# Causal masks, gain column sums and six groups of query products moved ahead in the two sparse-attention layers

## The chip, the core and the metric

One core of a Trainium2 chip runs the whole network in one launch. The metric is the device time of that core in microseconds (us). TensorE is called PE in the profile (PEld is its weight load), VectorE is DVE, ScalarE is ACT, GpSimd is POOL, and SP issues the DMAs.

## What is computed

The network has one layer of a first kind (local attention, pooling, gated feed-forward) and then two layers of a second kind. The change touches only the second kind. For 256 tokens of width 1024, cut to what matters:

```
proj = h @ w_in                      # qa, kva, kr, dq, dk, dv, iq, ik, iw
# multi-head latent attention, 8 heads of 64 + 32
q = rms_norm(qa) @ w_q_up            # rotary on the last 32
k_nope, v = rms_norm(kva) @ w_uk, rms_norm(kva) @ w_uv
out_a = softmax(mask(q k^T * 96**-0.5)) v
# sparse attention, 8 heads of 64, keys chosen by an indexer
score = sum over 8 index heads of iw * relu(iq ik^T * 32**-0.5)
score = where(key <= query, score, -inf);  sel = top_k(score, 64)
out_b = softmax(dq dk[sel]^T * 64**-0.5 - slope * distance) dv[sel]
x = layer_norm(ALPHA * x + [out_a, out_b] @ w_o)
# 16 experts, 2 of them for each token, chosen by sigmoid(x @ router_w)
x = layer_norm(ALPHA * x + experts(x))
```

`dq` is `h @ w_in[:, dq columns]`: these are the query products of the change. The router needs, for each expert, the sum over the features of gain times router weight and of shift times router weight: the column sums.

## The kernel before

Each engine has its own program, written out by hand, and semaphores order them. `w.next(name)` waits for one more count of a semaphore, `wait_ge` for a fixed count. Tokens stand in two halves of 128 rows. Weights come as float32 slabs, which ACT splits into a high part (`hi`) and DVE or POOL into a low part (`lo`); each product of two float32 numbers is then three fp32r matmuls (`products`, lines 2083 to 2087).

In each of the two layers PE does the following.

- It multiplies the input by `w_in` (`token_major`, slabs L_IN and L_IN_B), ACT and DVE save the result to `proj`, and PE turns the normalised latents (`feature_major`, line 2024: four chunks of 128 columns ahead, the fifth when the products reach it; a turn is a transposition with the identity, line 2010).
- It multiplies the latents by `w_q_up` (slabs L_QUP), `w_uk` and `w_uv`. Beside these run the turns of the indexer's inputs (`turn_b`) and the 16 score products of the indexer (`idx_score`, line 2379). ACT takes the relu of each (`idx_relu`, line 1028), and DVE adds it up into `score`, whose tile is `bias_h` (`idx_add`, line 1786).
- It turns `q_up` (tile `wide_a`) and `k_up` (tile `wide_b`) in four rounds of four plus four turns. ACT copies the queries to `q_t` (line 1058), DVE the keys to `k_t` (line 1815). A round's query turn waits for the query copy two rounds back, and its key turn for the key copy two rounds back.
- It computes the column sums, 8 matmuls of 128 x 32 in float32 (line 2413; in the trace x16, two passes each). DVE adds the causal masks to both halves of `score` (line 1820).
- It runs the first attention in 19 steps: step i issues the scores of unit i (line 2164), the flip of unit i-2, which is a turn of its probabilities, the weighing of unit i-3 (line 2180) and then what is put beside. A unit is a head and a half; units 0 to 7 have 128 keys, units 8 to 15 have 256. From step 4 on the query products for the second, sparse attention stand beside (`sparse_queries`): 32 groups of three matmuls with 256 columns, 2 or 3 groups in each step, written to banks 6 and 7.
- Each unit also costs DVE a round: `largest` (MAX8, line 1831), `logits` (line 1311) and `take` (line 1836). Eight rounds of largest and take choose the 64 keys of a half.
- Then come the sparse attention, the output projection, the router and the experts.

Who waits for whom at the change: `logits(i)` needs the score on PE; the exponential (line 849) needs the logits; flip i needs the exponential; weighing i needs ACT's copy of the turned probabilities (line 858), and ACT does that copy of unit i only after the exponential of unit i+2. POOL makes `router_gb` (router weight times gain and shift, line 719), which the column sums read.

Of the kernel before, what the change touches and what calls it, by code (L numbers as in the profile page):

```python
# [30 lines left out]
ALU = mybir.AluOpType  # L31
AX = mybir.AxisListType

P = 128
SEQ, D = 256, 1024
# [213 lines left out]
def build(nc, A, out):  # L249

    ctx = ExitStack()
    with ctx:
# [228 lines left out]
        N_IDX = HALVES * IDX_HEADS  # L481

# [155 lines left out]
        def _(pool):  # L638
# [42 lines left out]
            for layer in range(LAYERS):  # L681
                if layer == 0:
                    pool.wait_ge(S["x_updated"], 8)
                else:
                    pool.wait_ge(S["ln_done"], HALVES * layer)
                nc.gpsimd.memset(q_up[:, :, :, MLA_D:P], 0.0).then_inc(S["pads_zero"], 1)
# [29 lines left out]
                pool.wait_ge(S["columns_in"], 16)  # L716
                pool.wait_ge(S["router_in"], 16 * N_ROUTER)
                for g in range(2):
                    nc.gpsimd.tensor_tensor(router_gb[:, g], router_w[:],
                                            columns[:, layer, 0, g, :].unsqueeze(2).broadcast_to([P, DC, EXPERTS]), ALU.mult)  # L720
# [24 lines left out]
        def _(act):  # L745
# [253 lines left out]
            for layer in range(LAYERS):  # L999
# [31 lines left out]
                def save_qup(i):  # L1031
# [5 lines left out]
                              low=True, to=low_x)  # L1037
                splits_to(b + L_UK)
# [22 lines left out]
                w.next("gain_sums")  # L1061
                nc.scalar.copy(route[:, 4, :], bank[6][:, sums_at])
# [165 lines left out]
        def _(dve):  # L1228
# [520 lines left out]
            for layer in range(LAYERS):  # L1749
# [53 lines left out]
                w.next("idx_masked")  # L1803
                for i in range(N_IDX):
                    idx_add(i)
                    if i + 1 == IDX_AFTER_QUP:
                        save_qup(1)
# [197 lines left out]
        def _(pe):  # L2005
# [320 lines left out]
            for layer in range(LAYERS):  # L2326
# [20 lines left out]
                def turn_b(at):  # L2347

                    w.upto(("copied_even", "copied_odd")[at % 2], (4, 2)[at % 2] * layer + at // 2)
# [8 lines left out]
                def qup_first():  # L2358

                    groups[0] += 1  # L2360
                    if groups[0] == HALVES * QC // 2:
                        w.next("in_saved0", 3)
                        w.next("in_saved1", 3)
# [4 lines left out]
                def idx_score():  # L2368
# [3 lines left out]
                    if i == 0:  # L2372
                        w.next("copied_even", 2)
# [7 lines left out]

# [369 lines left out]
```

## Time and profile before

| what | value |
|---|---|
| median of 3 runs | 1110.01 us (1109.86 to 1110.74) |
| profiled execution | 1114.11 us |
| its span | 1112.2 us |
| PE busy | 1061.4 us, 95% of the span |
| DVE, ACT, POOL busy | 558.0, 437.5, 116.8 us |
| chain that ended last | PE 83%, DVE 6%, DMA 6%, ACT 3%, issue 2% |
| mean granted clock of PE | 0.976 |

The span is the time from the first instruction to the last of one execution; the device time of that execution is a little longer. All times of stretches and instructions below count from the span's start. A granted clock of 1.0 stands for 2.4 GHz, 0.5 for 1.2 GHz.

### The profile page before, as it was taken

The numbers are of one execution on the slowest core, as the hardware profiler recorded it, in microseconds if no ns is written. First come the engines' busy times: TensorE is split into PE (matmuls) and PEld (weight loads), VectorE is DVE, ScalarE is ACT, GpSimd is POOL, SyncE is SP. The second block draws the span as 40 slices with busy tenths as digits, with TensorE's granted clock in tenths as the row PEclk, the third lists the DMA queues.
The fourth block names the chain that finished last, engine by engine and source line by source line (L and its number), as shares of the span: only waits on it lengthen the run. The fifth ranks groups of instructions, "written<-read, shape, count | busy, mean of one in ns | idle before, by whom it ended". The sixth has DMA issues, their size and how long they took to land.

```text
span 1112.2 us, 16375 instructions
## 1 busy us (share of the span) xinstructions
PE 1061.4 (95%) x6290; PEld 741.5 (67%) x6290; DVE 558.0 (50%) x1071; ACT 437.5 (39%) x811; POOL 116.8 (11%) x129
## 2 busy tenths in 40 slices
PE   8999998999999998999999999989999999999995
PEld 5898987999999797886344443349797734444332
DVE  5764376676666667657322223265765642222224
ACT  5345454554554356644211121145555522112111
POOL 1200000000000025340000000022534000000000
PEclk9999998999999998999999999989899999999998
DMA  8843245555555354358999999935444989999993
GB/s 300 272 141 127 77 152 189 169 172 189 190 187 187 111 172 185 119 181 354 423 420 421 420 422 420 420 130 184 138 167 126 403 363 420 422 420 420 422 420 139
DMA packets 84877, 294.60 MB, mean 265 GB/s; under 512 B 6376, under 2 KB 45638, under 8 KB 60106
## 3 DMA queue, kind: packets, MB, share of 16 engines
q1 hardware_dynamic: 81936, 289.33, 68.1%
q10 hardware_dynamic: 2874, 4.36, 1.1%
q8 instruction: 44, 0.72, 0.3%
q14 instruction: 23, 0.19, 0.0%
HBM read 292.62 MB, written 1.05 MB: 264 GB/s over the span
## 4 chain that ended last, share of the span: by engine, by line
PE 83%; DVE 6%; DMA 6%; ACT 3%; issue 2%; SPq 0%; DVEq 0%; POOL 0%; ACTq 0%
PE bank L2569 17%; PE bank L2578 9%; PE bank L2085 8%; PE bank L2086 7%; PE bank L2087 7%; PE bank L2146 4%; PE bank L2148 4%; PE bank L2147 4%; PE bank L2010 4%; DMA raw<-in_w_in 3%; PE bank L2556 3%; DMA early_w<-in_w_up 3%; PE bank L2180 2%; PE bank L2601 2%; PE bank L2164 2%
## 5 line engine op out<-in xcount | busy, mean ns | idle before, releaser
L1236 DVE TENSOR_TENSOR lo<-raw,hi 128x2048 fp32r<-128x2048 f32 (+4 forms) x73 | 155.5, 2138 | 47.0 <-ACT hi L753 46.7
L753 ACT CAST hi<-raw 128x2048 fp32r<-128x2048 f32 (+5 forms) x74 | 132.1, 1791 | 45.2 <-PE bank L2087 41.4
L1488 DVE TENSOR_TENSOR proj<-bank,proj 64x512 f32<-64x512 f32 x32 | 34.6, 1082 | 210.4 <-PE bank L2591 210.4
L2146 PE MATMUL bank<-xs,hi 128*128 128x256 f32 x448 | 129.0, 288 | 3.6 <-DVE xs L1270 1.5
L2148 PE MATMUL bank<-xs,lo 128*128 128x256 f32 x448 | 127.9, 286 | 0.0
L2147 PE MATMUL bank<-xs,hi 128*128 128x256 f32 x448 | 127.9, 286 | 0.0
L2085 PE MATMUL bank<-hi,xs 128*128 128x512 f32 (+2 forms) x240 | 90.3, 376 | 4.7 <-DVE xs L1274 1.6
L1165 ACT ACTIVATE proj<-bank 64x512 f32<-64x512 f32 x32 | 18.8, 589 | 191.4 <-PE bank L2570 191.4
L2146 PEld LDWEIGHTS bank<-xs,hi 128*128 128x128 f32 x448 | 87.3, 195 | 5.0 <-issue 3.4
L2087 PE MATMUL bank<-lo,xs 128*128 128x512 f32 (+2 forms) x240 | 87.9, 366 | 0.0
L2086 PE MATMUL bank<-hi,xs 128*128 128x512 f32 (+2 forms) x240 | 87.8, 366 | 0.0
L2147 PEld LDWEIGHTS bank<-xs,hi 128*128 128x128 f32 x448 | 87.3, 195 | 0.4
L2148 PEld LDWEIGHTS bank<-xs,lo 128*128 128x128 f32 x448 | 87.2, 195 | 0.0
L658 POOL TENSOR_TENSOR lo<-raw,hi 128x512 fp32r<-128x512 f32 (+1 forms) x44 | 57.1, 1328 | 279.4 <-ACT hi L753 217.3
L2570 PE MATMUL bank<-moe_w,xg 128*64 128x512 f32 x160 | 70.3, 592 | 0.0
L1506 DVE SCALAR_TENSOR_TENSOR expert_out<-bank,slot_gate,expert_out 128x512 fp32r<-128x512 f32 x32 | 24.0, 750 | 88.7 <-ACT expert_out L1178 88.7
L649 POOL TENSOR_TENSOR stat<-stat,power 128x1 f32<-128x1 f32 (+2 forms) x15 | 16.5, 1098 | 476.7 <-DVE stat L1967 227.0
L1178 ACT ACTIVATE expert_out<-bank,slot_gate 128x512 fp32r<-128x512 f32 x32 | 22.0, 687 | 109.9 <-PE bank L2578 109.9
L1723 DVE SCALAR_TENSOR_TENSOR proj<-bank,conv,proj 128x255 f32<-128x255 f32 (+1 forms) x88 | 38.5, 478 | 49.3 <-ACT proj L977 46.4
L2578 PE MATMUL bank<-moe_w,act_t 128*64 128x512 f32 x256 | 59.8, 601 | 0.9 <-ACT act_t L1169 0.9
L849 ACT ACTIVATE prob<-logit,row_min 128x128 f32<-128x128 f32 (+1 forms) x80 | 36.5, 456 | 46.7 <-DVE row_min L1311 45.0
L2085 PEld LDWEIGHTS bank<-hi,xs 128*128 128x128 f32 x240 | 45.2, 188 | 10.8 <-issue 2.8
(306 smaller groups left out, 2398.0 us busy)
## 6 DMA issues: line engine op xcount, KB each, us to landing
raw<-in_w_up SPq DMA_DIRECT2D x34, 1024.0 KB, 5.1
moe_w<-in_w_down SPq DMA_DIRECT2D x32, 1024.0 KB, 19.5
raw<-in_w_in SPq DMA_DIRECT2D x20, 1024.0 KB, 5.6
moe_w<-in_w_up SPq DMA_DIRECT2D x20, 1024.0 KB, 20.9
raw<-in_w_down SPq DMA_DIRECT2D x19, 1024.0 KB, 5.1
early_w<-in_w_gate SPq DMA_DIRECT2D x12, 1024.0 KB, 18.7
early_w<-in_w_up SPq DMA_DIRECT2D x12, 1024.0 KB, 20.8
raw<-in_w_gate SPq DMA_DIRECT2D x10, 1024.0 KB, 16.2
```

What stands on the lines that cost most here:

```text
L658: ins = nc.gpsimd.tensor_tensor(low(n)[:, part], raw[:, n % RING, part], high(n)[:, part].bitcast(F32), ALU.subtract)
L753: nc.scalar.copy(high(n)[:, 0:size], raw[:, n % RING, 0:size]).then_inc(S["hi_done"], 1)
L1236: tt(low(n)[:, 0:size], raw[:, n % RING, 0:size], high(n)[:, 0:size].bitcast(F32), ALU.subtract).then_inc(S["lo_done"], 1)
L2085: mm(out_, lhs_hi, rhs_hi, start=first, stop=False)
L2086: mm(out_, lhs_lo, rhs_hi, start=False, stop=False)
L2087: return mm(out_, lhs_hi, rhs_lo, start=False, stop=last)
L2146: mm(dst, wh[:, k, col], x_hi, start=k == 0, stop=False)
L2147: mm(dst, wh[:, k, col], x_lo, start=False, stop=False)
L2148: ins = mm(dst, wl[:, k, col], x_hi, start=False, stop=k == k_chunks - 1)
L2569: mm(to[0:SLOTS, :], rows_[:, kk, :], gate[:, k, :], start=kk == 0, stop=kk == DC - 1)
L2570: ins = mm(to[SLOTS:P, :], rows_[:, kk, :], up[:, k, :], start=kk == 0, stop=kk == DC - 1)
L2578: ins = mm(to[SLOTS * c:SLOTS * (c + 1), :], act[:, kk, :], down[:, k, 512 * c:512 * (c + 1)], start=kk == 0, stop=kk == 3)
```

## The change

Four things move, in each of the two layers.

1. **Column sums.** PE issues them between the fourth and the fifth chunk of the latents' turns, ahead of the products with `w_q_up`; ACT copies them to `route` after the latents' copies and not after the query copies. POOL makes `router_gb` at the start of the layer, ahead of its memsets. The waits for `in_saved0`, `in_saved1` and `pads_zero` move with them.
2. **Causal masks.** DVE adds the first half's mask inside the indexer's additions, after the one with i = 8, and the second half's after round 1 of the first attention.
3. **Six groups of query products** stand among the turns: three after round 2 and three after round 3.
4. **The other 26 groups** stand beside steps 1 to 17 of the first attention, one or two in each, and none in step 18. The wait for the last relu, which stood ahead of the column sums, now stands ahead of the first turn.

```
+        GROUPS_BY_TURN = (0, 0, 3, 6)
POOL, start of a layer:
+                pool.wait_ge(S["columns_in"], 16)
+                pool.wait_ge(S["router_in"], 16 * N_ROUTER)
+                for g in range(2):
+                    nc.gpsimd.tensor_tensor(router_gb[:, g], router_w[:],
+                                            columns[:, layer, 0, g, :].unsqueeze(2).broadcast_to([P, DC, EXPERTS]), ALU.mult)
                 nc.gpsimd.memset(q_up[:, :, :, MLA_D:P], 0.0).then_inc(S["pads_zero"], 1)
...
ACT, after feature_major(QC + KVC, ...):
+                w.next("gain_sums")
+                nc.scalar.copy(route[:, 4, :], bank[6][:, sums_at]).then_inc(S["copied_even"], 1)
                 splits_to(b + L_UK)
...
DVE:
+                def causal(half):
+                    dst = score[:, half, 0:P * (half + 1)]
+                    tt(dst, dst, mask[:, half, 0:P * (half + 1)], ALU.add).then_inc(S["idx_masked"], 1)
                 for i in range(N_IDX):
                     idx_add(i)
+                    if i == IDX_HEADS:
+                        causal(0)
...
-                for half in range(HALVES):
-                    keys = P * (half + 1)
-                    dst = score[:, half, 0:keys]
-                    tt(dst, dst, mask[:, half, 0:keys], ALU.add).then_inc(S["idx_masked"], 1)
-                w.next("idx_masked", HALVES)
                 def largest(i):
+                    if i % HEADS == 0:
+                        w.next("idx_masked")
                 def take(i):
+                    if i == 1:
+                        causal(1)
...
PE:
+                w.next("in_saved0", 3)
+                w.next("in_saved1", 3)
+                w.next("pads_zero", 2)
+                for k in range(DC):
+                    ins = mm(bank[6][:, sums_at]..., router_gb[:, :, k, :], start=k == 0, stop=k == DC - 1)
+                ins.then_inc(S["gain_sums"], 1)
                 token_major(b + L_QUP, 1, QC, [4 * MLA_D], qup[0], lhs=low_x, ready=fm_chunk, between=qup_first)
...
                 w.next("idx_relu", N_IDX)
                 for i in range(4):
                     for src, to, copied in ((q_up, q_turned(i), "copied_q"), (k_up, k_turned(i), "copied_k")):
...
+                    sparse_queries(GROUPS_BY_TURN[i])
...
                 attention(...,
-                          beside=lambda i: sparse_queries(i) if i > 3 else None)
+                          beside=lambda i: sparse_queries(6 + 26 * i // 17 if i < 17 else 2 * 2 * DC))
```

The number given to `sparse_queries` is now how many groups have been issued in all; before, it was `2 * 2 * DC * (i - 3) // 15`, thus 2 groups at a step and 3 at steps 11 and 18.

On PE, before: the last two rounds of turns (`wide_a` queries, `wide_b` keys), the column sums and the first scores (`k_t,q_t`).

```order
L2010 MATMUL bank<-const,wide_b 128x128 [waits copied_k]
L2010 MATMUL bank<-const,wide_b 128x128 x3
L2010 MATMUL bank<-const,wide_a 128x128 [waits copied_q]
L2010 MATMUL bank<-const,wide_a 128x128 x3
L2010 MATMUL bank<-const,wide_b 128x128 [waits copied_k]
L2010 MATMUL bank<-const,wide_b 128x128 x3
L2413 MATMUL bank<-router_gb,const 128x32 [waits idx_relu,kv_saved1,kv_saved0]
L2413 MATMUL bank<-router_gb,const 128x32 x7
L2164 MATMUL bank<-k_t,q_t 128x128 [waits copied_k,copied_q]
L2164 MATMUL bank<-k_t,q_t 128x128
L2164 MATMUL bank<-k_t,q_t 128x128 [waits logits]
```

On PE, now: round 3's key turn is followed by three groups of query products (`xs,hi` and `xs,lo`), and then by the first score.

```order
L2015 MATMUL bank<-const,wide_b 128x128 [waits copied_k]
L2015 MATMUL bank<-const,wide_b 128x128 x3
L2090 MATMUL bank<-xs,hi 128x256
L2091 MATMUL bank<-xs,lo 128x256
L2092 MATMUL bank<-xs,hi 128x256
L2090 MATMUL bank<-xs,hi 128x256
L2091 MATMUL bank<-xs,lo 128x256
L2092 MATMUL bank<-xs,hi 128x256
L2090 MATMUL bank<-xs,hi 128x256
L2091 MATMUL bank<-xs,lo 128x256
L2092 MATMUL bank<-xs,hi 128x256
L2169 MATMUL bank<-k_t,q_t 128x128 [waits copied_q,copied_k,kv_saved1,kv_saved0]
```

Three more groups stand ahead of round 3 in the same way, and the column sums are gone from here. On PE, before, at the latents' turns (`const,xn`) ahead of the products with `w_q_up` (`hi,low_x`):

```order
L2010 MATMUL bank<-const,xn 128x128 [waits fm_lo]
L2010 MATMUL bank<-const,xn 128x128 x3
L2010 MATMUL bank<-const,xn 128x128 [waits fm_lo,lo_done]
L2010 MATMUL bank<-const,xn 128x128
L2085 MATMUL bank<-hi,low_x 128x384 [waits fm_lo]
```

and now:

```order
L2015 MATMUL bank<-const,xn 128x128 [waits fm_lo]
L2015 MATMUL bank<-const,xn 128x128 x3
L2389 MATMUL bank<-router_gb,const 128x32 [waits pads_zero,in_saved1,in_saved0]
L2389 MATMUL bank<-router_gb,const 128x32 x7
L2015 MATMUL bank<-const,xn 128x128 [waits fm_lo,lo_done]
L2015 MATMUL bank<-const,xn 128x128
L2090 MATMUL bank<-hi,low_x 128x384 [waits fm_lo]
```

The column sums (`router_gb,const`) stand between the fourth and the fifth chunk. On DVE, before, from the key copies to the first logits (`bias_h<-bias_h,const` are the masks, ISA is the logits' instruction):

```order
L1815 COPY k_t<-bank 128x512 [waits turned_a,idx_added]
L1815 COPY k_t<-bank 128x512 [waits turned_a] x3
L1820 TENSOR_TENSOR bias_h<-bias_h,const 128x128
L1820 TENSOR_TENSOR bias_h<-bias_h,const 128x256
L1831 MAX power<-bias_h 128x8 [waits idx_masked]
L1311 ISA logit,row_min<-bank,const 128x128 [waits probs,scores]
```

and now:

```order
L1824 COPY k_t<-bank 128x512 [waits turned_a,idx_added]
L1824 COPY k_t<-bank 128x512 [waits turned_a] x3
L1834 MAX power<-bias_h 128x8 [waits idx_masked]
L1312 ISA logit,row_min<-bank,const 128x128 [waits probs,scores]
```

No mask addition is left between the last key copy and the first largest.

## Rows read from the trace of the kernel before

**Rows 1.** The page, part 2: granted clock of TensorE in 40 slices, tenths.
```profile
PEclk9999998999999998999999999989899999999998
```

**Rows 2.** Busy time in stretches: both turn-and-attention stages, their slow parts, experts.
```profile
core 0: us, PE busy (x) PEld busy (x) DVE busy (x) ACT busy (x) POOL busy (x), PEclk, DMA share, GB/s
424.80:462.56 37.76, 34.25 (x250) 32.02 (x248) 26.82 (x97) 22.40 (x68) 16.16 (x14) 0.91 0.51 196
791.47:830.93 39.46, 37.17 (x250) 34.87 (x248) 26.32 (x97) 22.29 (x68) 16.10 (x14) 0.83 0.50 187
434.40:441.30 6.90, 6.40 (x29) 5.80 (x29) 4.27 (x26) 4.12 (x18) 0.00 (x0) 0.52 0.97 383
796.40:810.00 13.60, 13.15 (x60) 12.20 (x58) 8.03 (x36) 6.55 (x21) 3.49 (x3) 0.50 0.83 311
520.00:526.00 6.00, 6.00 (x29) 2.03 (x30) 5.68 (x17) 1.44 (x2) 0.00 (x0) 1.00 0.42 122
526.00:730.00 204.00, 201.14 (x1054) 80.91 (x1050) 53.77 (x102) 39.02 (x73) 0.15 (x1) 1.00 1.01 419
```

**Rows 3.** Timeline of PE, layer 0: start, duration, instructions, [idle before <-releaser].
```profile
402.50 1.25 PE L2010 MATMUL bank<-const,xn 128*128 128x128 f32 x10
404.94 0.44 PE L2085 MATMUL bank<-hi,low_x 128*128 128x384 f32 x1 [1.18 <-DVE low_x L1274]
...
429.19 0.66 PE L2010 MATMUL bank<-const,wide_b 128*128 128x128 f32 x4 [1.21 <-DVE k_t L1815]
429.69 0.60 PE L2010 MATMUL bank<-const,wide_a 128*128 128x128 f32 x4
...
430.56 1.87 PE L2413 MATMUL bank<-router_gb,const 128*128 128x32 f32 x16
432.27 0.69 PE L2164 MATMUL bank<-k_t,q_t 128*128 128x128 f32 x4
434.13 0.49 PE L2164 MATMUL bank<-k_t,q_t 128*128 128x128 f32 x2 [1.18 <-DVE row_min L1311]
```

**Rows 4.** Timeline of PE, layer 0, inside the first attention.
```profile
439.33 0.63 PE L2164 MATMUL bank<-k_t,q_t 128*128 128x128 f32 x2
...
441.60 0.38 PE L2164 MATMUL bank<-k_t,q_t 128*128 128x128 f32 x2
...
442.07 0.37 PE L2085 MATMUL bank<-xs,hi 128*128 128x256 f32 x1
...
442.87 0.39 PE L2164 MATMUL bank<-k_t,q_t 128*128 128x128 f32 x2
...
449.70 0.36 PE L2085 MATMUL bank<-xs,hi 128*128 128x256 f32 x1
...
450.85 0.60 PE L2164 MATMUL bank<-k_t,q_t 128*128 128x256 f32 x2
```

**Rows 5.** Timeline of PE, layer 1: the fourth turn of the queries.
```profile
796.37 0.95 PE L2010 MATMUL bank<-const,wide_a 128*128 128x128 f32 x4
```

**Rows 6.** Timeline of DVE, layer 0: indexer, key copies, masks, first rounds.
```profile
419.80 0.92 DVE L1786 SCALAR_TENSOR_TENSOR bias_h<-logit,idx_w,bias_h 128x256 f32<-128x256 f32 x1 [0.77 <-ACT logit L1028]
...
428.45 1.29 DVE L1815 COPY k_t<-bank 128x512 f32<-128x512 f32 x2
...
431.37 2.19 DVE L1820 TENSOR_TENSOR bias_h<-bias_h,const 128x128 f32<-128x128 f32 x2
433.59 0.29 DVE L1831 MAX8 power<-bias_h 128x8 f32<-128x128 f32 x1
...
434.38 0.29 DVE L1831 MAX8 power<-bias_h 128x8 f32<-128x128 f32 x1
```

**Rows 7.** All instructions of line 1820 (mask additions): ns minimum/median/maximum.
```profile
L1820 DVE TENSOR_TENSOR bias_h<-bias_h,const x4: 411/1003/1483, 431.4 to 800.0; 128x128 f32<-128x128 f32 x2, 128x256 f32<-128x256 f32 x2
```

**Rows 8.** Timeline of ACT, layer 0: the last relu of the indexer.
```profile
425.87 0.41 ACT L1028 ACTIVATE logit<-bank 128x256 f32<-128x256 f32 x1
```

**Rows 9.** Timeline of POOL, layer 0: after its three memsets.
```profile
396.55 1.01 POOL L649 TENSOR_TENSOR stat<-stat,power 128x4 f32<-128x4 f32 x1 [18.45 <-DVE stat L1257]
```

More of the change, by code:

```diff
@@ L715, in _ @@
                     .then_inc(S["kr_spread"], 1)
[L716 to L720, printed above, removed]
                 w.next("qup_saved0", 2)
@@ L1060, in _ @@
                     w.skip("turned_a")
-                w.next("gain_sums")
-                nc.scalar.copy(route[:, 4, :], bank[6][:, sums_at])
                 def sparse_queries(i):
@@ L2347, in turn_b @@
                 def turn_b(at):
-                    w.upto(("copied_even", "copied_odd")[at % 2], (4, 2)[at % 2] * layer + at // 2)
+                    w.upto(("copied_even", "copied_odd")[at % 2], (5 * layer + 1, 2 * layer)[at % 2] + at // 2)
                     for c in range(2):
@@ L2361, in qup_first @@
                     if groups[0] == HALVES * QC // 2:
-                        w.next("in_saved0", 3)
-                        w.next("in_saved1", 3)
                         w.next("staged", 6)
@@ L2372, in idx_score @@
                     if i == 0:
-                        w.next("copied_even", 2)
+                        w.next("copied_even", 3)
                         w.next("copied_odd", 2)
@@ L2398, in _, with sparse_queries @@
                 w.next("kr_spread")
-                w.next("pads_zero", 2)
-                for i in range(4):
-                    for src, to, copied in ((q_up, q_turned(i), "copied_q"), (k_up, k_turned(i), "copied_k")):
-                        w.upto(copied, 4 * layer + i - 1 if i else 0)
-                        for c in range(2):
-                            for half in range(HALVES):
-                                at = c * SEQ + half * P
-                                ins = turn(to[:, at:at + P], src[:, half, 2 * i + c, :])
-                        ins.then_inc(S["turned_a"], 1)
-                w.next("kv_saved0")
-                w.next("kv_saved1")
-                w.next("idx_relu", N_IDX)
-                for k in range(DC):
-                    ins = mm(bank[6][:, sums_at].rearrange("p (g e) -> p g e", g=2), const[:, C_ONE:C_ONE + 1].broadcast_to([P, P]),
-                             router_gb[:, :, k, :], start=k == 0, stop=k == DC - 1)
-                ins.then_inc(S["gain_sums"], 1)
-                w.next("copied_q", 4)
-                w.next("copied_k", 4)
+                w.next("idx_relu", N_IDX)
                 asked = [0]
-                def sparse_queries(i):
-                    groups_by = 2 * 2 * DC * (i - 3) // 15
+                def sparse_queries(groups_by):
                     while asked[0] < groups_by:
@@ L2435, in sparse_queries @@
                             ins.then_inc(S["slab_used"], 1)
+                for i in range(4):
+                    for src, to, copied in ((q_up, q_turned(i), "copied_q"), (k_up, k_turned(i), "copied_k")):
+                        w.upto(copied, 4 * layer + i - 1 if i else 0)
+                        for c in range(2):
+                            for half in range(HALVES):
+                                at = c * SEQ + half * P
+                                ins = turn(to[:, at:at + P], src[:, half, 2 * i + c, :])
+                        ins.then_inc(S["turned_a"], 1)
+                    sparse_queries(GROUPS_BY_TURN[i])
+                w.next("kv_saved0")
+                w.next("kv_saved1")
+                w.next("copied_q", 4)
+                w.next("copied_k", 4)
                 attention(lambda h, half: q_t[:, h, half * P:(half + 1) * P],
```

2 lines of the change are left out of this document (added).

## The prediction

> **What bounds the kernel now.** I read the page first, then the stretches, then the timelines of the engines around the change. On the page the reader is to see TensorE's granted clock dip in a few slices of an otherwise full row [rows 1]. The stretches tell where: in each layer from the first turn of `q_up` to the first score of the sparse attention, 37.76 us in layer 0 and 39.46 us in layer 1 [rows 2]. Inside them the clock is 0.52 for 6.90 us in layer 0 and 0.50 for 13.60 us in layer 1, that is 1.2 in place of 2.4 GHz. PE counts as busy for 34.25 and 37.17 us there, DVE for 26.8 and 26.3, ACT for 22.4 and 22.3. So PE's own stream sets the length, plus its waits, plus what the low clock costs.
>
> The waits lie early [rows 3]. The third round's key turn waits 1.21 us for DVE's key copy; the third score, at 434.13, waits 1.18 us for the logits, since DVE does both masks (2.19 us) before the first largest [rows 6]; and no product group is there to fill until step 4. With the narrow column sums (430.56 to 432.27) this makes ten microseconds in which the array does little.
>
> After these stages come the experts, fed by weights at 419 GB/s with the DMA engines at 1.01 [rows 2]. That looks like a cover under which a gain could vanish. It is not: from 520 to 526 us the DMAs run at 0.42, 122 GB/s, because all slots are full and wait for PE. The stream starts again when PE starts the experts, so what PE gains before carries through.
>
> **The change part by part, on PE, for one layer.** I build up the length of the stretch anew.
>
> (a) First turn to end of round 2: 4.9 us, as before. Before it is 424.80 to 429.69 and 791.47 to 796.37 [rows 2, 3, 5]. The wait for the last relu now stands ahead of the first turn, and that relu ends at 426.28 [rows 8], 1.5 us after the first turn of now. It costs nothing, for the round-2 key turn waits anyway for DVE's first key copy, started at 428.45 after the last addition [rows 6]; a set of four turns takes 0.44 (two sets from 429.69 to 430.56), so the five sets ahead of that key turn, begun at 426.3, end at 428.5, still before the copy does. Without that cover it would cost up to 1.5.
>
> (b) Three groups, round 3, three groups. Three groups take 1.15 us (449.70 to 450.85), two take 0.80 (442.07 to 442.87) [rows 4], thus 0.355 a group and 0.09 a burst. Round 3 takes 0.87 [rows 3]. Sum 3.17. The last key copy of DVE (0.69, half of the 1.29 for two) is hidden by the second three.
>
> (c) Steps 0 to 4. A step of 128 keys without its groups is 441.60 to 442.07, 0.47: score 0.22, flip 0.11, weighing 0.14. Five scores, three flips and two weighings are 1.7 us, the six groups in four bursts 2.5. Then there is a wait: weighing 0 needs ACT's copy, which stands behind the exponential of unit 2. From the first score, DVE needs about 0.43 to the first logits, two rounds of 0.79 (433.59 to 434.38) and the second half's mask, 0.41 at its shortest [rows 6, 7], with the next largest and logits 0.5; ACT adds some 0.9. That is 3.8 us, against 2.5 of work that PE has until there. I take 1.4 of waiting; the bounds are 0.5 (DVE's parts overlap PE's) and 2.5. Sum 5.6.
>
> (d) Steps 5 to 18. Steps 6 to 18 took 441.60 to 462.56, 20.96 us at full clock with 28 groups in 13 bursts. Now they hold 19 in 12: less 9 x 0.355 and 0.09, 17.7. Step 5 with one group is 0.9. Sum 18.6.
>
> (e) Waits of the leaner steps. A step with one group of 128 keys is 0.91, hardly longer than DVE's 0.79, and DVE also saves the first half's heads in between. DVE's 26.8 us of work must now fit in some 33. I take 1.0, from bounds 0 (it all fits) and 2.0.
>
> The stretch becomes 4.9 + 3.2 + 5.6 + 18.6 + 1.0 = 33.3 us.
>
> (f) Column sums, new place. The latents' turns end at 403.75 and the product waits 1.18 us for `low_x` [rows 3]. The sums take 1.71 us (430.56 to 432.27), start when eight of the ten turns are out, and push the last two and the product to about 405.3 from 404.94: 0.4 us, from bounds 0 and 1.7. Behind PE here stand ACT's and DVE's copies of the fifth chunk, then the splits of `w_uk`: 0.8 us later in the worst case, while their slab is first needed some ten microseconds on. ACT's small copy of the sums (0.2) is in the same gap.
>
> (g) First mask inside the additions: DVE stands idle 0.77 us before the next addition [rows 6], and and that addition takes 0.92 while POOL rotates. I take 0, from bounds 0 and 1.1 (half of the 2.19 for two).
>
> (h) POOL's two products ahead of its memsets: after the memsets POOL is idle for 18.45 us [rows 9]; nothing. In layer 0 they wait for a small load (128 x 64 numbers) that SP issues right after the first kind of layer ends; the same idle time covers it. SP's later loads wait for low parts and turns that move with PE.
>
> So layer 0 goes from 37.76 to 33.7, a gain of 4.1, and layer 1 from 39.46 to 33.7, a gain of 5.7: together 9.8 us. The sum is made against the profiled execution (1114.11 us, span 1112.2), which is 4.1 us above the median of the runs; taken from the median, 1110.0 - 9.8 = **1100.2 us**. Roughly half of it is waiting that is filled; the rest is that 20 us at half clock disappear. That last part is a choice. Before each fall of the clock PE had issued turns with waits between, and in layer 0 then the column sums and the first scores; the clock rose again after the products came back, at 441.3 and 810.0. Now two bursts of three groups stand there.
>
> A rule speaks against counting on this. The row first: in layer 1 the clock had fallen by 796.4, and ahead of it stood turns with no wait longer than 1.2 us. The Trainium skill, "TensorE: Matmul & The Clock Gate", table "Why this matters for your kernels", asks only that long idle gaps between bursts be avoided; by it the clock would never have fallen here, and the trace disagrees. The same page, "Part 4: PE-mode transpose", says that a transposition does not count as PE work for the clock in the way a matmul does. By that rule the trace agrees, and it is the second rival below: the turns of (a) are all still there.
>
> **The rivals.**
>
> *B. The clock still falls among the turns.* For: (a) keeps its turns and its waits, and in layer 1 the fall came before any of the new groups. Against: in layer 0 it came only at 434.4, long after such turns, so some products nearby are enough to hold it. Price: a step with two groups took 439.33 to 441.60, 2.27, at the low clock, 1.27 at the full one [rows 4]; a slow stretch of 6.90 us full of products so costs 3.0. In one layer 1103.2, in both 1106.2 us.
>
> *C. The chain of the softmax, not PE, is the length.* If units pass at DVE's and ACT's pace, 26 groups beside run no faster than 32 did, and the six ahead only push the first score: 3.2 us after round 2 in place of 2.6 (429.69 to 432.27), plus the 0.4 of (f), thus 1.0 later in each layer. Result 1112.1, slower. It decides if steps 5 to 18 shrink by less than 1 us. Against: from step 6 on PE is never idle before.
>
> *D. The gain is given back.* The weight stream ends when it did, since the slots' loads take their time from something that did not move. Result 1110.0. Against: the 0.42 from 520 to 526. That the change does not do what it says is no case: the order on PE shows the groups and sums moved.
>
> **How the numbers follow.** Forecast 0.58; B 0.28 (mostly in one layer); C 0.04; D 0.06; the rest, 0.04, is a gain above the bounds. Within the forecast, (c), (e) and (f) at their good ends give 2.3 us a layer more, at their bad ends 2.8 less; they will not all fall on one side, so I take some 3 us down and 4 up, and B reaches to 1106.2: range 1097.0 to 1106.5. A measurement of this kernel can tell 0.2%, 2.2 us, from no change. Faster by more: 0.90. Within: 0.06. Slower: 0.04.
>
> **What would show it.** In the profile after: the two stretches at about 33.7 us each; a granted clock of 1.0 through both; column sums right behind eight latents' turns, with the product after them 0.4 us late; no wait for `k_t` after round 3; one wait of about 1.4 us at the first weighing; the sparse attention's first score right behind the last weighing; experts of the same length as before. It is wrong if a stretch shows 0.5 for several microseconds (B), if steps 5 to 18 show waits for `row_min` or `prob_t` of more than 2 us in sum (C), or if the experts start early and end as late as before (D).

## The result and the profile after

The change makes the kernel faster: a median of 1104.19 us over six runs (1101.22 to 1105.70), beside 1110.6 us for the kernel before (six runs, 1109.86 to 1116.77). The ratio is 0.9921, with a 95% interval of 0.9903 to 0.9940. The forecast was 1100.2 with a range of 1097.0 to 1106.5. The profiled execution of the changed kernel took 1101.22 us, its span is 1099.4.

On the page of the changed kernel PE is busy for 1050.7 us, 96% of the span (before 1061.4), DVE for 556.7, ACT for 437.7, POOL for 117.3. Its row of the clock answers to [rows 1]: no slice but the last is below nine tenths.

```profile
PEclk9999999999999999999999999999999999999998
```

From here on I measure each layer from a mark that lies ahead of the turns and of all that changed its order behind them: from the start of the indexer's last six scores to the first score of the sparse attention. Only the column sums and the first mask now stand ahead of that mark. The first turn stands 1.61 us behind that mark before. These are the two stretches before, and below them the section between them (columns as in [rows 2]):

```profile
423.19:462.56 39.37, 35.82 (x256) 33.03 (x254) 28.28 (x98) 23.77 (x71) 17.77 (x15) 0.91 0.49 188
789.87:830.93 41.06, 38.73 (x256) 35.88 (x254) 27.43 (x98) 23.65 (x71) 17.70 (x15) 0.83 0.48 180
462.56:789.87 327.31, 317.61 (x1704) 173.40 (x1703) 133.78 (x296) 102.05 (x215) 36.55 (x47) 0.98 0.82 329
```

The same of the changed kernel, and with them the end of the routing and the experts of layer 0:

```profile
424.05:458.47 34.42, 31.62 (x239) 28.45 (x238) 26.32 (x97) 23.86 (x71) 16.61 (x14) 1.00 0.57 215
784.16:818.49 34.33, 31.60 (x239) 28.43 (x238) 25.99 (x97) 23.88 (x71) 16.62 (x14) 1.00 0.59 215
458.47:784.16 325.69, 316.25 (x1718) 174.30 (x1719) 134.25 (x297) 102.07 (x216) 37.84 (x48) 0.99 0.83 331
516.00:522.00 6.00, 6.00 (x30) 2.00 (x30) 5.76 (x17) 1.31 (x2) 0.00 (x0) 1.00 0.44 126
522.00:726.00 204.00, 201.12 (x1054) 80.89 (x1050) 53.70 (x102) 38.84 (x73) 0.00 (x0) 1.00 1.01 418
```

The reader is to see three things. The granted clock is 1.00 in both stretches, where it was 0.91 and 0.83. The stretches are 4.95 and 6.73 us shorter, 11.7 together; the column sums, which left them, cost 0.41 a layer at their new place, so the two layers bring 10.9 us. The spans of this pair differ by 12.8 us. The rest, 1.9 us, is less than what executions of one kernel differ by outside these stretches: the section between them took 327.31 us before and 325.69 now, and in a second execution of each kernel (both in the experiments) 324.93 before and 328.01 now. Last, the experts [rows 2] took 204 us then and now, and the DMAs ran at 0.44 and 126 GB/s just ahead of them: the gain of layer 0 went through.

In the timeline of PE after, layer 0, around the turns and the first units, compare [rows 3]:

```profile
405.64 0.42 PE L2015 MATMUL bank<-const,xn 128*128 128x128 f32 x2
...
424.05 1.77 PE L2382 MATMUL bank<-gates 128*128 128x256 f32 x6
427.27 0.63 PE L2015 MATMUL bank<-const,wide_a 128*128 128x128 f32 x4 [1.46 <-ACT logit L1029]
...
430.03 0.66 PE L2015 MATMUL bank<-const,wide_b 128*128 128x128 f32 x4 [0.38 <-DVE k_t L1824]
430.44 0.36 PE L2090 MATMUL bank<-xs,hi 128*128 128x256 f32 x1
...
433.54 0.65 PE L2169 MATMUL bank<-k_t,q_t 128*128 128x128 f32 x4
...
436.83 0.43 PE L2185 MATMUL bank<-value,prob_t 128*128 128x64 f32 x2 [0.57 <-ACT prob_t L859]
...
438.78 0.39 PE L2169 MATMUL bank<-k_t,q_t 128*128 128x128 f32 x2
```

PE now waits 1.46 us for the last relu ahead of the first turn. The wait for a key copy is down to 0.38 us, from 1.21. The third score follows the first two with one group between them and no wait, where it waited 1.18. At the first weighing PE waits 0.57.

### The profile page after: what moved, and what is told of

It reads as the page before. It is cut to its first block, busy times and chain, and to the rows that moved or that the text cites. A ratio compares the mean times of both kernels' runs of the same rounds, so it can differ in the third digit from the quotient of the medians.

```text
span 1099.4 us, 16372 instructions
## 1 busy us (share of the span) xinstructions
PE 1050.7 (96%) x6286; PEld 731.1 (66%) x6290; DVE 556.7 (51%) x1071; ACT 437.7 (40%) x811; POOL 117.3 (11%) x129
## 4 chain that ended last, share of the span: by engine, by line
PE 71%; DMA 5%; DVE 5%; issue 1%; ACT 1%; SPq 0%; DVEq 0%; ACTq 0%
PE bank L2574 17%; PE bank L2583 9%; PE bank L2090 6%; PE bank L2091 6%; PE bank L2092 6%; PE bank L2151 4%; PE bank L2153 4%; PE bank L2152 4%; PE bank L2015 3%; PE bank L2561 3%; DMA raw<-in_w_in 3%; DMA early_w<-in_w_up 3%; PE bank L2606 2%; PE bank L2185 2%; PE bank L2169 2%
```

## The experiments

A stretch below is the one just defined, a pair of numbers is layer 0 and layer 1, and the clock is the one granted in it. All kernels compute the whole result. What is called masks, sums and groups are the three parts of the change: the causal masks moved into the additions and rounds; the column sums moved ahead of the product with `w_q_up`; six groups placed among the turns and 26 beside the units from the first on.

| kernel | median us | ratio to before, 95% | stretches us | clock |
|---|---|---|---|---|
| before (profiled first) | 1110.01 | | 39.37 / 41.06 | 0.91 / 0.83 |
| before, once more | 1110.18, one execution | | 38.98 / 39.49 | 0.91 / 0.91 |
| the change | 1104.19 | 0.9921 [0.9903, 0.9940] | 34.42 / 34.33 | 1.00 / 1.00 |
| the change, once more | 1103.30 | 0.9904 [0.9882, 0.9926] | 34.42 / 34.36 | 1.00 / 1.00 |
| masks only | 1115.24 | 0.9999 [0.9977, 1.0021] | 38.71 / 41.15 | 0.91 / 0.83 |
| sums only | 1113.17 | 0.9983 [0.9967, 0.9999] | 40.22 / 39.10 | 0.83 / 0.91 |
| masks and sums | 1108.89 | 0.9938 [0.9920, 0.9956] | 35.79 / 37.20 | 1.00 / 0.95 |
| groups only | 1105.49 | 0.9912 [0.9885, 0.9938] | 36.49 / 36.41 | 1.00 / 1.00 |
| masks and groups | 1107.67 | 0.9936 [0.9910, 0.9962] | 36.51 / 36.40 | 1.00 / 1.00 |
| sums and groups | 1103.10 | 0.9899 [0.9870, 0.9929] | 35.04 / 34.95 | 1.00 / 1.00 |
| before with idle matmuls | 1108.40 | 0.9952 [0.9933, 0.9971] | 37.39 / 37.30 | 1.00 / 1.00 |
| no groups among the turns | 1103.10 | 0.9906 [0.9879, 0.9934] | 34.34 / 34.24 | 1.00 / 1.00 |
| first groups in the key wait | 1101.45 | 0.9886 [0.9859, 0.9913] | 33.55 / 33.44 | 1.00 / 1.00 |
| and groups by step | 1100.56 | 0.9875 [0.9844, 0.9905] | 33.03 / 32.95 | 1.00 / 1.00 |

Each ratio is taken against executions of the kernel before that ran beside that kernel, and these were not alike: their median is 1114.14 us for masks, sums, both and groups alone, 1113.02 for the idle matmuls, the two versions with groups at other places ("no groups among the turns", "first groups in the key wait") and the change once more, and 1113.68 for the rest. That is why 1115.24 goes with 0.9999. The medians alone don't order the kernels: executions of the changed kernel scatter by 4.5 us, of the kernel before by 7, of "masks only" by 10. A stretch at full clock repeats within 0.03 us (34.42 and 34.42, 34.33 and 34.36), so differences below a microsecond are read from the stretches.

**Masks only.** Of the change, only this part, in the kernel before:

```
 for i in range(N_IDX):
     idx_add(i)
+    if i == IDX_HEADS:
+        causal(0)
...
-for half in range(HALVES):
-    ... tt(dst, dst, mask[:, half, 0:keys], ALU.add)
-w.next("idx_masked", HALVES)
...
 def take(i):
     ...
+    if i == 1:
+        causal(1)
```

> The kernel before with only the causal masks moved. Theory A (three things stand ahead of the attention and end within a microsecond of each other: PE's column sums, DVE's masks, ACT's table load, which follows the copy of the sums): the masks alone give at most 0.3 us a layer, since the first exponential still waits for the table load until 433.9; time within 1 us of before, and the clock falls as before. Theory B (the masks were what the first scores waited for, 1.2 us): 1.2 us less in each layer, about 2.4 us faster.

Measured: ratio 0.9999, stretches within 0.7 us of before's, the clock as before. DVE was free earlier, but its work found the next engine busy. ACT in layer 0 of this kernel (start, duration, instruction):

```profile
434.23 0.18 ACT L1062 COPY route<-bank 128x32 f32<-128x32 f32 x1 [1.56 <-PE bank L2420]
434.42 1.28 ACT L849 ACT_TABLE_LOAD   x1
435.71 0.40 ACT L849 ACTIVATE prob<-logit,row_min 128x128 f32<-128x128 f32 x1
```

ACT can't load the exponential's table before it has copied the column sums, and those come last on PE. The load takes 1.28 us, and PE's first flip waits 0.88 for the exponential behind it. A wait for DVE has become one for ACT.

**Sums only.** The column sums and their copy at the new place, masks, turns and groups as before (the relu wait back behind the turns, groups from step 4 on):

```
-    sparse_queries(GROUPS_BY_TURN[i])
...
-beside=lambda i: sparse_queries(6 + 26 * i // 17 if i < 17 else 2 * 2 * DC)
+beside=lambda i: sparse_queries(2 * 2 * DC * (i - 3) // 15) if i > 3 else None
...
+causal(0)
+causal(1)
+w.next("idx_masked", HALVES)
```

> The kernel before with only the column sums moved ahead of the query-latent products. Theory A: PE is ready for the first score earlier but DVE is not (masks end at 433.6); the stretch gains nothing and 0.4 us is added ahead of it: 0 to 1 us slower than before in all. Theory B (PE's stream is the length, so 1.71 us of sums leaves it and 0.4 comes back): 1.3 us less in each layer, about 2.6 us faster.

Measured: ratio 0.9983, at most 0.3% of gain, where a little loss was expected. Now the masks hold: between the last key copy and the first logits on DVE the two take 1.30 us in layer 0 and 2.18 in layer 1, and there PE waits 1.85 us for the logits. At the full clock of its layer 1 the part ahead of the attention is 8.42 us, 0.66 shorter than the 9.08 in layer 0 of before. The product with `w_q_up` starts 2.85 us behind the latents' first turn, 2.44 before: the new place costs 0.41.

**Masks and sums,** that is the change without its groups (the second diff without its last three lines).

> Masks and column sums moved, the query products as before (from step 4). Theory A: together they free the start of the attention, first score to fifth score 0.8 to 1.7 us earlier in each layer; the clock still falls in at least one layer, since nothing wide stands there: 1.5 to 3.5 us faster than before, and the groups are worth the other 4 to 6 us of the change. Theory C (the groups are worth little): as fast as the changed kernel within 1 us.

Measured: ratio 0.9938, some 7 us, twice the upper end of what was expected. Neither part did much alone; together they bring a stretch of 35.79 at full clock:

```profile
425.89:461.68 35.79, 31.97 (x240) 28.67 (x238) 26.45 (x97) 23.58 (x70) 17.73 (x15) 1.00 0.56 207
789.15:826.35 37.20, 33.38 (x239) 30.16 (x238) 26.10 (x97) 23.58 (x70) 17.72 (x15) 0.95 0.53 199
```

And with no group of products before step 4 the clock held in layer 0; in layer 1 it fell only 12 us behind the mark, for some 3.5 us.

**Groups only.** Turns and groups as in the change, masks as before. The sums stay behind the turns, but in bank 7 on PE and ACT, since bank 6 now holds products of a group:

```
-    nc.scalar.copy(route[:, 4, :], bank[6][:, sums_at])
+    nc.scalar.copy(route[:, 4, :], bank[7][:, sums_at])
...
+w.next("idx_relu", N_IDX)
...
         ins.then_inc(S["turned_a"], 1)
+    sparse_queries((0, 0, 3, 6)[i])
```

> The query products moved as in the change, column sums (in bank 7) and masks at their old places. Theory A: the clock holds through both stretches and the products fill; the masks' 2.2 us on DVE and the sums' 1.7 us on PE stay ahead of the first scores, so each stretch is 1.5 to 2.5 us longer than in the changed kernel: 4 to 6 us faster than before. Theory C: within 2 us of before.

Measured: ratio 0.9912, stretches 36.49 and 36.41 at full clock. The stretches are longer than the change's by what was expected; the gain over before, 9 to 10 us, is larger than the 4 to 6 expected. This part alone carries most of what a median shows. The two parts that did next to nothing in the kernel before are worth another 2.1 us of the stretch with it, 1.7 net of the sums' 0.41.

**Before with idle matmuls.** The order of the work is untouched, but for the relu wait, which now stands ahead of the key turn of round 2; bf16 matmuls on zeros into bank 7, whose result nobody reads, fill PE's waits:

```
+    if i == 2 and src is k_up:
+        w.next("idx_relu", N_IDX)
+        busy(5, bank[7])
     w.upto(copied, 4 * layer + i - 1 if i else 0)
...
+busy(2, bank[7])
 w.next("kv_saved0")
 w.next("kv_saved1")
-w.next("idx_relu", N_IDX)
...
-beside=lambda i: sparse_queries(i) if i > 3 else None)
+beside=lambda i: sparse_queries(i) if i > 3 else busy((0, 4, 2, 2)[i], bank[7]))
```

> The kernel before with nothing moved, but idle matmuls of 512 bf16 columns on zeros in PE's waits: 5 ahead of the round-2 key turn, 2 after the turns, and 4, 2 and 2 beside steps 1 to 3 of the first attention (bank 7, not read). Theory A (half of the change's gain is the clock, held by wide matmuls in this place): granted clock 1.0 in both stretches, layer 1's stretch 3 to 5 us shorter, layer 0's 1 to 2.5, in all 3 to 6 us faster than before. Theory B (the clock is not governed by what stands here): the clock falls as before, 0 to 2 us slower.

Measured: ratio 0.9952. The stretches of this kernel, then the first burst of layer 0 (the trace has four of its five matmuls) and the key turn behind it, which no longer waits:

```profile
425.10:462.49 37.39, 35.81 (x268) 31.78 (x269) 28.28 (x98) 23.76 (x71) 17.76 (x15) 1.00 0.53 198
788.58:825.88 37.30, 35.73 (x269) 31.79 (x270) 27.93 (x98) 23.77 (x71) 17.77 (x15) 1.00 0.53 198
```
```profile
429.94 1.03 PE L2201 MATMUL bank<-zeros 128*128 128x512 bf16 x4
431.10 0.66 PE L2010 MATMUL bank<-const,wide_b 128*128 128x128 f32 x4
```

Work that computes nothing takes 1.98 and 3.76 us off the stretches. So whether the clock falls in them hangs on what PE does in its early waits. This run doesn't tell whether it is the waiting that costs the clock or the lack of such matmuls: both changed at once. Some 0.4 us of the idle work lands on the path (the first score comes 9.50 us behind the mark, 9.08 before), so the order of before at full clock is 37.0 to 37.4 us. With it the two shares of this pair of profiles separate: of 10.9 us, the clock gave some 2.0 to 2.4 in layer 0 and 3.8 to 4.1 in layer 1; the order of the work gave 2.2 to 2.6 in each.

**No groups among the turns.** The change with all 32 groups beside the steps:

```
-GROUPS_BY_TURN = (0, 0, 3, 6)
+GROUPS_BY_TURN = (0, 0, 0, 0)
...
-beside=lambda i: sparse_queries(6 + 26 * i // 17 if i < 17 else 2 * 2 * DC)
+beside=lambda i: sparse_queries(2 * 2 * DC * (i + 1) // 18 if i < 17 else 2 * 2 * DC)
```

> The changed kernel without the six groups among the turns: all 32 groups beside steps 0 to 17, one or two in each. Theory A (the groups' gain is that they begin before step 4 at all, and the clock): steps 0 to 3 now take them and the turns lose 2.3 us, so the stretch is the same within 0.5 us if the clock holds; if it falls in layer 1, as it did behind the turns before, 2 to 3.5 us are lost there. Theory D (the place among the turns matters by itself): 1 to 2 us longer in each layer at full clock.

Measured: ratio 0.9906, and the stretches are those of the change, 0.1 us shorter:

```profile
422.27:456.61 34.34, 31.32 (x240) 28.33 (x238) 26.35 (x97) 23.88 (x71) 16.62 (x14) 1.00 0.59 216
782.84:817.08 34.24, 31.21 (x240) 28.32 (x238) 25.99 (x97) 23.89 (x71) 16.61 (x14) 1.00 0.58 216
```

The two bursts of three groups among the turns, which the diff shows most prominently, are neither needed for the clock nor do they save anything. The first score comes 1.1 us earlier without them, and the attention takes 1.0 longer.

**First groups in the key wait.** The last relu and the first three groups stand between the query and the key turn of round 2, so that the relu wait no longer holds the first turn and the groups fill the wait for the key copy:

```
-w.next("idx_relu", N_IDX)
...
+            if i == 2 and src is k_up:
+                w.next("idx_relu", N_IDX)
+                sparse_queries(GROUPS_BY_TURN[2])
...
-    sparse_queries(GROUPS_BY_TURN[i])
+    if i == 3:
+        sparse_queries(GROUPS_BY_TURN[3])
```

> The changed kernel with the relu wait moved behind the first five turn sets and the first three groups put between the query and the key turns of round 2, where PE waited for the key copy. Theory A (PE's stream plus its waits is the length; POOL's low part of the slab is there in time): 0.8 to 1.2 us shorter in each layer, 1.6 to 2.4 us faster than the changed kernel. Rival: the low part or the relu holds the groups and with them the key turn, so DVE's last copies come later and nothing is gained, or 0.5 us is lost.

Measured: ratio 0.9886, the stretches 0.87 and 0.89 us shorter than the change's, all of it ahead of the first score (8.59 us behind the mark, not 9.49).

**The change once more,** for the scatter.

> The changed kernel once more, to see where its runs differ (1101.2 to 1105.7). Theory A: the turn-and-attention stretches are the same within 0.3 us at full clock; what differs is the granted clock, in one of these stretches or at the transitions (before the first layer's end, before the experts, between the layers), 1 to 4 us. Rival: the difference is in the weight stream of the experts at full clock.

Measured: 1103.30 us, ratio 0.9904, the stretches within 0.03 us. The section between the two stretches and the window from 720 to 740 us in it, here and then in the first profile:

```profile
457.48:785.49 328.01, 317.32 (x1718) 174.90 (x1719) 135.00 (x297) 102.14 (x216) 37.88 (x48) 0.98 0.82 328
720.00:740.00 20.00, 16.74 (x67) 7.43 (x64) 11.17 (x25) 8.05 (x10) 7.89 (x11) 0.74 0.37 131
```
```profile
720.00:740.00 20.00, 15.82 (x75) 7.62 (x77) 12.93 (x30) 9.75 (x13) 8.37 (x11) 0.91 0.43 155
```

The section is 2.3 us longer than in the first profile, and the clock in the window is 0.74, not 0.91: executions of one kernel differ by where the clock falls outside these stretches.

**Masks and groups; sums and groups.** The first is "groups only" with the first diff; the second is the change with `causal(0)` and `causal(1)` behind the key copies.

> Masks and groups moved, column sums at their old place (bank 7). Theory A (the sums' 1.71 us lie on PE's stream, and the table load behind their copy holds the first exponential; the masks matter only once the sums are gone): the stretch from the indexer's last six scores to the sparse attention is as long as with the groups alone, 36.4 us, within 0.3. Rival (the masks are worth their 1.2 us of waiting by themselves): 35.2 to 35.6.

> Column sums and groups moved, masks at their old place behind the last key copy. Theory A: the two mask additions (0.8 to 2.2 us on DVE, by how much POOL still runs) now hold the first logits, while one group fills only 0.4: the stretch is 34.9 to 36.0 where the changed kernel has 34.4. Rival (the groups hide the masks): 34.4 within 0.2.

Measured, layer 0 of each, masks and groups first:

```profile
425.87:462.38 36.51, 33.40 (x256) 30.22 (x254) 26.46 (x97) 23.99 (x72) 16.64 (x14) 1.00 0.54 203
```
```profile
422.85:457.89 35.04, 31.80 (x240) 28.45 (x238) 27.31 (x98) 23.89 (x71) 16.62 (x14) 1.00 0.57 211
```

At full clock throughout, the parts can be priced. With the sums at their old place, moving the masks is worth 0.0 (36.49 and 36.51); with them moved, 0.6 (35.04 to 34.42). Moving the sums is worth 2.1 of the stretch if the masks are moved (36.51 to 34.42) and 1.45 if not (36.49 to 35.04), less the 0.41 in each. Of the 2.1, 1.72 is PE time ahead of the first score (11.21 to 9.49 us) and the rest is the table load: in "groups only", too, it stands behind the copy of the sums and the first exponential starts 1.7 us after the first score (436.10 and 434.41), where it takes 0.8 in the change (434.34 and 433.54).

**Groups by step.** The kernel of "first groups in the key wait", with the other 26 groups spread by hand, more of them where PE waited:

```
+BY_STEP = (0, 1, 4, 0, 1, 1, 2, 1, 2, 1, 2, 1, 2, 1, 2, 2, 2, 1, 0)
...
-beside=lambda i: sparse_queries(6 + 26 * i // 17 if i < 17 else 2 * 2 * DC))
+beside=lambda i: sparse_queries(6 + sum(BY_STEP[:i + 1])))
```

> As the version with groups in the round-2 wait, and the other 26 groups by a table: four at step 2 and none at step 3, two at step 15 and one at step 17, to fill the waits of 0.57 us at the first weighing and 0.27 at the fourteenth. Theory A: 33.0 to 33.3 us a stretch in place of 33.5; time 0.4 to 1 us less, which runs whose clock differs elsewhere may hide. Rival: four groups at step 2 hold score 3 and with it DVE, 33.5 or more.

Measured: median 1100.56 us, ratio 0.9875 [0.9844, 0.9905], stretches 33.03 and 32.95. These are all of PE's waits from the first turn to step 5 of layer 0:

```profile
430.10 0.66 PE L2016 MATMUL bank<-const,wide_a 128*128 128x128 f32 x4 [0.62 <-ACT q_t L1062]
...
431.05 0.36 PE L2091 MATMUL bank<-xs,hi 128*128 128x256 f32 x1 [0.29 <-POOL lo L660]
...
438.97 0.44 PE L2186 MATMUL bank<-value,prob_t 128*128 128x64 f32 x2 [0.29 <-ACT prob_t L860]
```

Of 33.03 us PE is busy for 31.70; little is left to fill here. By its stretches it beats the change by 1.4 us in each layer; the intervals of the two ratios overlap, so the medians alone don't show it.

**Before once more,** one execution.

> The kernel before once more. Theory A (its two stretches differ from run to run only by where the clock falls, with everything else repeating): a stretch without a fall of the clock would be 37.2 to 37.5 us; with 6.8 us at half clock 39 to 40, with 13.6 us about 41; its time lies 6 to 12 us over the changed kernel's. Rival: the stretches differ at the same clock.

Measured: 1110.18 us; the stretches and the section between them:

```profile
423.64:462.62 38.98, 35.48 (x256) 32.85 (x255) 28.30 (x98) 23.77 (x71) 17.78 (x15) 0.91 0.51 190
787.55:827.04 39.49, 35.91 (x256) 33.08 (x255) 27.96 (x98) 23.76 (x71) 17.80 (x15) 0.91 0.50 187
462.62:787.55 324.93, 314.50 (x1701) 172.37 (x1702) 132.79 (x296) 102.04 (x215) 36.54 (x47) 0.99 0.83 331
```

The low clock comes back in both layers, but in layer 1 it lasts much less long than in the execution on which the prediction was built (0.91, not 0.83), and the stretch is 1.57 us shorter.

## Why the prediction was right, and where it was not

The forecast case came true: faster by more than 0.2%, the clock at 1.00 in both stretches, experts of the same length. Its terms, against the trace of the changed kernel, layer 0. The first turn would have come at 425.66, had it not waited for the relu (the mark, 424.05, plus the 1.61 of before).

| term | predicted | measured |
|---|---|---|
| (a) first turn to end of round 2 | 4.9 | 425.66 to 430.44, 4.78 |
| (b) two bursts and round 3 | 3.17 | 430.44 to 433.54, 3.10 |
| (c) steps 0 to 4 | 5.6 | 433.54 to 438.78, 5.24 |
| (d), (e) steps 5 to 18 and their waits | 19.6 | 438.78 to 458.47, 19.69 |
| sum | 33.3 | 32.81 |
| (f) column sums at the new place | 0.4 | 0.41 |

**(a)** The relu wait did stand on PE for 1.46 us, and it did cost nothing: the key turn of round 2, which waited 1.21 us before [rows 3], now waits 0.38. DVE's key copies set that point. "First groups in the key wait" shows what was left on the table: with the groups in that wait the same part is 0.9 shorter.

**(c)** The wait at the first weighing is 0.57 us, not the 1.4 taken, near the low bound of 0.5. The terms of the chain that were too large can be read on DVE and ACT:

```profile
433.27 0.28 DVE L1834 MAX8 power<-bias_h 128x8 f32<-128x128 f32 x1
434.00 0.29 DVE L1312 CUSTOM_DVE_ANT_0 logit<-bank,const 128x128 f32<-128x128 f32 x1 [0.44 <-PE bank L2169]
...
435.28 0.42 DVE L1809 TENSOR_TENSOR bias_h<-bias_h,const 128x256 f32<-128x256 f32 x1
```
```profile
432.83 1.28 ACT L850 ACT_TABLE_LOAD   x1
434.34 0.40 ACT L850 ACTIVATE prob<-logit,row_min 128x128 f32<-128x128 f32 x1 [0.22 <-DVE row_min L1312]
...
436.53 0.24 ACT L859 COPY prob_t<-bank 128x128 f32<-128x128 f32 x1
```

The first logits start 0.46 us after the first score (433.54), as taken. The third start at 435.81, after two rounds and the mask: 1.81, where the sum had 1.99. From there to the weighing at 436.83 it is 1.02, where "the next largest and logits 0.5; ACT adds some 0.9" made 1.4, since ACT's parts overlap DVE's. That is 3.29 us in place of 3.8, and PE's work in it is 2.72 in place of 2.5. The table load isn't on this chain: it stands at 432.83 now, behind the last query copy, and is over when the logits come. The prediction priced the move of the sums on PE alone and never named this load. It is why the move of the sums is worth more than PE's 1.7 us, and why the masks are worth nothing without it; the sum came out right since (c) was built up anew, from scratch, for the order in which all parts are there.

**(d) and (e)** The one named wait of PE behind step 5 is 0.27 us; what the leaner steps cost beyond that can't be told from PE's work in the trace. Together they are 0.1 off.

**(g)** The first mask takes 0.71 us in layer 1, and the next addition starts as it ends:

```profile
779.64 0.35 DVE L1784 TENSOR_SCALAR bias_h<-logit,idx_w 128x256 f32<-128x256 f32 x1 [0.42 <-ACT logit L1029]
780.03 0.71 DVE L1809 TENSOR_TENSOR bias_h<-bias_h,const 128x128 f32<-128x128 f32 x1
780.69 0.99 DVE L1787 SCALAR_TENSOR_TENSOR bias_h<-logit,idx_w,bias_h 128x256 f32<-128x256 f32 x1
```

It fits the 0.77 us gap [rows 6]: 0, as taken. **(h)** POOL's two products and memsets run from 377.94 us on, and no wait for `pads_zero` shows: 0, as taken.

**The gain, taken from the median.** Here the prediction went wrong, by a step of its own: "taken from the median, 1110.0 - 9.8". The 9.8 was worked out against an execution of 1114.11 us, and from there it would have given 1104.3, beside the 1104.19 measured. The 1110.0 was the median of three executions, and they were short ones: of the 40 executions of the kernel before that ran beside the experiments, on three chips, 39 took longer (1109.84 to 1116.97 us); whether the chip or chance made the first three short stays open. Against its share of the 40, the change once more brought 0.9904, some 10.7 us. A part of the 9.8, of the 5.7 in layer 1 above all, was the time at low clock of the profiled execution. "Before once more" ran in 1110.18 with a layer 1 that had 1.57 us less to lose and a layer 0 with 0.39 less; its stretches against the change's, less 0.41 each, give 8.9 us, not 10.9. So the size of the gain was right within what the clock of the kernel before varies by, and the number was 4 us low because it started too low. That 1104.19 still lies in the range is luck: no term of the range stands for the starting point, and its room upward was taken for bad ends of the terms and for rival B, none of which came. The bad ends of (c), (e) and (f) also add up to 3.4 us a layer (1.1, 1.0 and 1.3), not to 2.8; nothing came near them.

**Why the clock holds.** That the clock would hold came true, but not for the reason given, that "two bursts of three groups stand there". Those bursts aren't needed: without them, with the groups beginning beside step 0, the clock is 1.00 as well ("no groups among the turns"). What the runs show is a count. In the nine profiles with query products before step 4 or with idle matmuls, all 18 stretches ran at 1.00. In the five without (before twice, masks only, sums only, masks and sums) the clock fell in nine of ten. So added matmuls early in the stretch keep it; how much of them it takes stays open, and so does whether it is the filled waits or the matmuls themselves. All the turns stand in every one of these kernels, so the turns alone don't bring the fall. The next rows run from the mark, the first three of them to about where the clock fell:

```profile
789.87:796.40 6.53, 4.65 (x32) 3.62 (x31) 5.93 (x7) 4.91 (x11) 6.45 (x6) 1.00 0.05 5
787.55:799.50 11.95, 8.84 (x63) 7.31 (x62) 10.94 (x21) 7.68 (x17) 10.02 (x8) 1.00 0.33 99
423.89:430.40 6.51, 4.64 (x31) 3.61 (x30) 6.26 (x7) 4.92 (x11) 6.43 (x6) 0.99 0.11 14
425.89:437.60 11.71, 7.91 (x49) 5.78 (x47) 10.61 (x27) 8.41 (x20) 9.96 (x8) 1.00 0.35 99
```

They are layer 1 of before, layer 1 of "before once more", layer 0 of "sums only" and layer 0 of "masks and sums", where it did not fall. The first two are one and the same program, and the clock goes some 6.5 us behind the mark in one execution and some 12 in the other. "Sums only" loses it right behind waits of 0.62 and 1.21 us, which "masks and sums" (0.62 and 1.22) and layer 0 of before (0.62 and 1.21) pass at full clock; the changed kernel waits 1.46 and 0.38 among the same turns, as long in sum, and keeps it. PE was busy for 71 to 74% of the time ahead of these falls and for 68% of it in "masks and sums". So neither the longest wait nor the sum of the waits nor the busy share tells a fall, and one profile of a kernel doesn't tell what the clock does in its other executions. The Trainium skill, "TensorE: Matmul & The Clock Gate", "Why this matters for your kernels", names only long idle gaps as what drops the clock in mid-kernel; that row alone would not have foretold falls of the kernel before, where no wait ahead of them is longer than 1.23 us, and the traces disagree with it here as the prediction said.

**The rivals.** B (the clock falls among the turns): did not come in any of the eight profiles of kernels with the groups moved. C (the softmax chain): steps 6 to 18 went from 20.96 us to 18.77 (439.70 to 458.47), near the forecast, and PE's one named wait in them is 0.27. D (the gain given back in the weight stream): 0.44 and 126 GB/s ahead of the experts, and 204 us for them as before. "Roughly half" of the gain by waiting filled and half by the clock: 4.4 to 5.1 us of order against 5.8 to 6.5 of clock in this pair of profiles.

## What to carry to other kernels

Price a part of a change with the others in place: in the kernel before, masks or sums alone brought 0.2% or less and both together 0.6%; with the groups in place the masks alone are worth 0.0 us a layer, the sums alone 1.0 and both 1.7. Each freed an engine while another still held the work up, and one link was a table load that no wait in the program names. Separate a gain of order from a gain of clock by filling the waits with work that computes nothing; the filled kernel gives the full-clock length of the old order. And subtract a gain from the execution it was worked out on, not from a median of three: a few executions can all be short ones.

## What the runs showed of the hardware

- In the kernel before, the granted clock falls to 0.5 behind 6.5 to 12 us in which PE was busy for 71 to 74% of the time and never waited longer than 1.23 us. The same program lost it at different places in two executions. Bursts of two to five bf16 matmuls with 512 columns in its waits (four take 1.03 us) kept it at 1.00 in both stretches.
- The scatter of the whole kernel from run to run follows the clock. Of the 40 executions of the kernel before, the fifteen shortest (up to 1112.46 us) ran at a mean granted clock of 0.981 to 0.987, the fifteen longest (1115.63 and more) at 0.975 to 0.978. Stretches at full clock repeat within 0.03 us.
- DVE's additions with two inputs take much longer while POOL works. The next rows are DVE's in the changed kernel, in layer 0; POOL rotates from 417.54 us on and stood idle for 11.82 before:

```profile
415.70 0.35 DVE L1787 SCALAR_TENSOR_TENSOR bias_h<-logit,idx_w,bias_h 128x128 f32<-128x128 f32 x1 [0.40 <-ACT logit L1029]
...
418.29 0.82 DVE L1787 SCALAR_TENSOR_TENSOR bias_h<-logit,idx_w,bias_h 128x128 f32<-128x128 f32 x1 [0.64 <-ACT logit L1029]
```

The same addition takes 0.35 us beside an idle POOL and 0.82 beside a busy one. So do the masks: the one of 128x256 takes 0.42 at 435.28, when POOL's last product is over, and up to 1.48 before [rows 7], where POOL splits weights beside it. The Trainium skill, "SBUF — State Buffer", "SBUF: two separate sides", says that DVE and GpSimd have one port pair in common that one of them holds for a whole instruction, and names DVE operations with two inputs from SBUF among those that need it; the trace agrees. The second mask, where it stands now, comes when POOL is done.
